# Hybrid decoder step on one core: two weight blocks kept for the late gates, and the first late gate moved ahead of two embeddings

## The reference, cut to what matters

```python
h = h + (p_l @ w_ple) * jax.nn.sigmoid(rmsnorm(h, g_ple) @ w_ple_gate)
...
y_prompt = rmsnorm(hp, g_final)
y_sample = rmsnorm(hs, g_final)
```

## Time and profile before

| what | value |
|---|---|
| runs | 2041.95, 2042.4, 2044.65 us; median 2042.4 us |
| profiled execution: its own time | 2045.19 us |
| its span (first to last instruction) | 2043.4 us |
| mean granted TensorE clock | 0.993 of full speed |
| TensorE matmul, busy share of the span | 98% |
| VectorE, ScalarE, GpSimd | 42%, 21%, 32% |
| gate pass with embeddings and output, from about | 1908 us to the end |

### The profile page before, as it was taken

The page is one execution under the profiler, slowest core; times in us unless marked ns, Lnnn a source line. Parts: engine busy times, 40 slices in busy tenths (PEclk is TensorE's granted clock), DMA queues, the critical chain, the costliest instruction groups (busy, mean ns, idle before and its releaser), DMA issues. The chain is left out here.

```text
span 2043.4 us, 34180 instructions
## 1 busy us (share of the span) xinstructions
PE 2005.5 (98%) x12890; PEld 1973.0 (97%) x12890; DVE 865.3 (42%) x1353; ACT 435.9 (21%) x842; POOL 663.4 (32%) x427
## 2 busy tenths in 40 slices
PE   7999999999999999999999999999999999999998
PEld 7999999989999999999999999999999999999998
DVE  4110434447256555644566543114212411344557
ACT  4111333321111222222232222002101200221312
POOL 5322232213322222224363232323232323232434
PEclk8999999999999999999999999999999999999999
DMA  7232122117444555577644111111111111111313
GB/s 199 75 92 52 37 63 63 57 44 206 114 139 133 152 163 166 176 131 220 196 133 161 44 42 52 41 52 41 52 41 51 41 51 41 51 42 51 104 50 128
DMA packets 251066, 191.43 MB, mean 94 GB/s; under 512 B 19116, under 2 KB 221976, under 8 KB 250594
## 3 DMA queue, kind: packets, MB, share of 16 engines
q1 hardware_dynamic: 241858, 172.27, 29.6%
q10 hardware_dynamic: 9120, 17.93, 2.8%
HBM read 157.10 MB, written 33.09 MB: 93 GB/s over the span
## 5 line engine op out<-in xcount | busy, mean ns | idle before, releaser
L142 PE MATMUL acc<-x_hi,w_hi 128*128 128x344 f32 x2496 | 809.0, 324 | 6.8 <-PEq L499 3.3
L142 PE MATMUL acc<-x_hi,w_lo 128*128 128x344 f32 x2496 | 799.2, 320 | 0.0
L142 PE MATMUL acc<-x_lo,w_hi 128*128 128x344 f32 x2496 | 798.9, 320 | 0.0
L112 POOL TENSOR_SCALAR w_hi<-w_raw 128x1024 fp32r<-128x1024 f32 (+1 forms) x176 | 182.6, 1037 | 1167.7 <-PE acc L142 995.3
L142 PEld LDWEIGHTS acc<-x_hi,w_hi 128*128 128x128 f32 x2496 | 471.1, 189 | 8.8 <-issue 7.7
L142 PEld LDWEIGHTS acc<-x_lo,w_hi 128*128 128x128 f32 x2496 | 470.9, 189 | 0.0
L142 PEld LDWEIGHTS acc<-x_hi,w_lo 128*128 128x128 f32 x2496 | 470.7, 189 | 0.0
L115 POOL TENSOR_TENSOR w_lo<-w_raw,w_hi 128x1024 fp32r<-128x1024 f32 (+1 forms) x176 | 411.6, 2338 | 14.7
L142 PE MATMUL acc<-z_hi,w_hi 128*128 128x344 f32 x768 | 245.9, 320 | 0.0
L142 PE MATMUL acc<-z_hi,w_lo 128*128 128x344 f32 x768 | 245.3, 319 | 0.0
L142 PE MATMUL acc<-z_lo,w_hi 128*128 128x344 f32 x768 | 245.1, 319 | 0.0
(11 more groups left out here) (297 smaller groups left out, 2060.2 us busy)
## 6 DMA issues: line engine op xcount, KB each, us to landing
w_raw<-in_w_in SPq DMA_DIRECT2D x64, 512.0 KB, 4.3
page<-in_cache_k SPq DMA_DIRECT2D x64, 256.0 KB, 3.0
page<-in_cache_v SPq DMA_DIRECT2D x64, 256.0 KB, 2.7
w_raw<-in_w_up SPq DMA_DIRECT2D x32, 512.0 KB, 4.0
w_raw<-in_w_down SPq DMA_DIRECT2D x32, 512.0 KB, 3.6
merge_gate<-merge_gates SPq DMA_DIRECT2D x22, 516.0 KB, 3.8
merge_gates<-gate_out ACTq DMA_DIRECT2D x18, 516.0 KB, 3.6
w_raw<-in_w_ple_gate SPq DMA_DIRECT2D x16, 512.0 KB, 3.6
```

The lines of the kernel that those rows point to most:

```text
L112: nc.gpsimd.tensor_scalar(k.w_hi[:, par, 0:kb, :], k.w_raw[:, par, 0:kb, :], 1.0, 1.0, ALU.mult, ALU.mult).then_inc(k.w_rounded, 1)
L142: mm = k.nc.tensor.matmul(k.acc[:, c, 0:CW], w[:, par, i, :], x[:, i, cols], start=(i == 0 and j == 0), stop=(i == kb - 1 and j == 2))
```

## The change

The early pass ends with blocks 6 and 7 in the two weight buffers. The late pass now takes the blocks in the order 6, 7, 0, 1, 2, 3, 4, 5, so that units 16 and 17 use what lies there, and blocks 0 to 5 are loaded again as j = 8 to 13. Two loads and two splits fall away. Block 8 is split behind gate 16, block 9 behind gate 17 (before: behind gates 13 and 15). Gate 16 is placed ahead of embeddings 14 and 15 on TensorE. VectorE's and ScalarE's lists stay as they are, but for the two conditions that ask whether a unit is the first of its columns, which now go by the unit's number. On SyncE's queue the loads of j = 10, 11 and 12 stand ahead of the first store, that of j = 13 between the first and the second. The last turning of tiles takes blocks 4, 6 and 7 first and block 5, the last one now, at the end.

```diff
-LATE = [(m, 2) for m in range(KD)]
+LATE_ORDER = [KD - 2, KD - 1] + list(range(KD - 2))
+LATE = [(m, 2) for m in LATE_ORDER]
...
             for m in range(KD):
-                if m + 2 < KD:
+                if m + 4 < KD:
                     gate_weights(KD + m + 2)
                 if m >= 2:
                     store(m - 2)
...
-            for j in range(2, 2 * KD):
-                pool.wait_ge(s["g_ready"], 2 * (j - 1) if j - 2 < KD else NE + j - 1 - KD)
+            for j in range(2, 2 * KD - 2):
+                pool.wait_ge(s["g_ready"], 2 * (j - 1) if j < KD else NE + j - KD + 1)
                 split_landed(k, pool, e0 + j, j % 2, (e0 + j) // 2)
...
-                j = m if u < NE else KD + m
+                j = m if u < NE + 2 else KD + m
...
+            gates(NE)
             embed(NE - 2)
             embed(NE - 1)
             for m in range(KD):
-                gates(NE + m)
+                if m:
+                    gates(NE + m)
...
+            LAST = LATE_ORDER[KD - 1:]
+            SECOND = [b for b in range(4, KD) if b not in LAST]
...
-            turn_half(pt[:, 0, :], a, range(4, KD - 1))
+            turn_half(pt[:, 0, :], a, SECOND)
...
-            turn_half(pt[:, 0, :], a, range(KD - 1, KD))
+            turn_half(pt[:, 0, :], a, LAST)
...
-                if m == 0:
+                if u < 2 or u == NE:
                     nc.vector.tensor_copy(sq3[:, cols], squares3[:, cols]).then_inc(s["sq_summed"], 1)
...
-                if m:
+                if u >= 2 and u != NE:
                     act.wait_ge(s["sq_summed"], same_columns_before(u) + 1)
```

More of the change, by code:

```diff
@@ L2089, in tensor @@
             pe.wait_ge(s["y_ready"], 2 * EARLY_TILES)
-            turn_half(pt[:, 0, :], a, range(4, KD - 1))
-            turn_half(pt[:, 1, :], b_, range(4, KD - 1))
+            turn_half(pt[:, 0, :], a, SECOND)
+            turn_half(pt[:, 1, :], b_, SECOND)
             pe.wait_ge(s["scaled"], NG)
-            turn_half(k.acc[:, 1, :], TB, range(4, KD - 1))
+            turn_half(k.acc[:, 1, :], TB, SECOND)
             pe.wait_ge(s["added"], NG)
-            turn_half(pt[:, 0, :], a, range(KD - 1, KD))
-            turn_half(pt[:, 1, :], b_, range(KD - 1, KD))
-            turn_half(k.acc[:, 1, :], TB, range(KD - 1, KD)).then_inc(s["half_turned"], 1)
+            turn_half(pt[:, 0, :], a, LAST)
+            turn_half(pt[:, 1, :], b_, LAST)
+            turn_half(k.acc[:, 1, :], TB, LAST).then_inc(s["half_turned"], 1)
             pe.wait_ge(s["sq_summed"], NG)
```

## The result

The changed kernel takes 2047.39 us (median of 20 runs) beside 2043.63 for the kernel before (20 runs); the ratio is 1.0018, with a 95% interval from 1.0012 to 1.0025. It is 2.5 to 5.1 us slower, where 0.9 slower was forecast. One of the changed kernel's 20 runs, 3302.13 us at a mean granted clock of 0.555, is left out of the ratio; without it the median is 2047.11.

A forecast was written before the change was run, and what follows sets the result against it. TensorE is busy nearly throughout; only two pauses, caused by a serial VectorE and ScalarE chain, can be won back. Chain +0.74, clock +0.7, late pass -0.5 gave +0.9: 2043.3 us for the median, range 2040.5 to 2045.8.

The forecast's parts named there:

- The steps of the chain: VectorE and ScalarE's serial work on units 12 to 15: 1.86 us won, 0.6 and 2.16 lost, token sums 0.74 later.
- Gate 16 without a wait: On TensorE, gate 16 follows embedding 13 at 1987.95 and runs until 1990.85, its weights and bank being ready.
- no pause before embedding 15: On TensorE, the 2.75 us wait for the product of unit 13 is gone.
- add 12 at 0.56: On VectorE, the add of unit 12 takes 0.56 in place of 2.42 without block 9's split: 1.86 us won.
- product 14 late: On VectorE, the product of unit 14 waits for its later embedding and starts at 1992.15 instead of 1991.56: 0.6 lost.
- add 14 held: On VectorE, block 8's w_lo half on GpSimd holds the add of unit 14 until 1995.46: 2.16 us lost.
- the token sums 0.71 later: On TensorE, the token sums start at 1998.86 where they started at 1998.12: 0.74 us later.
- a pause of 5.00: TensorE waits once before the token sums, from 1993.85 to 1998.86: 5.0 us instead of 2.75 and 1.28.
- The late pass: Fewer loads, in a new queue order, cut TensorE's 1.0 us wait for the y output: 0.5 won, ends 0 and 1.0.
- The clock's term: Low clock from 1998.0 costs the token sums 0.7 and gate 17 still 1.40: net +0.7, ends -1.4 and +2.9.
- rival 2: Slower: the 5.0 us pause keeps the clock low through token sums and all of gate 17: +3.6, 2046.0; chance 0.16.
- a cold gate 18: On TensorE, gate 18 also starts at the low clock: another 2.9, so 2048.9; thought unlikely.

The follow-up runs named there:

- e4: The changed kernel with block 8 split only behind the sum of unit 15; 2044.63 us, ratio 0.9998 to the kernel before.
- e1: The changed kernel's new block order, with gate 16 put back behind embedding 15; 2042.47 us, ratio 0.9991 to the kernel before.
- e2: The kernel before, in its old block order, with gate 16 moved ahead of embeddings 14 and 15; 2048.07 us, ratio 1.0019 to the kernel before.
- e5: The changed kernel with gate 17 moved ahead of the wait for the token sums; 2045.25 us, ratio 1.0011 to the kernel before.
- e11: The kernel before with gate 17 moved ahead of the wait for the token sums, nothing else; 2042.43 us, ratio 0.9996 to the kernel before.

## Why the prediction was wrong

- **The steps of the chain held.** Gate 16 without a wait, no pause before embedding 15, add 12 at 0.56, product 14 late (0.50 of waiting, 0.6 forecast), add 14 held (2.69 us from its start, 2.72 forecast), the token sums 0.71 later (0.74 forecast), a pause of 5.00 (5.0 forecast). e4 and e1 show the w_lo half as what holds add 14, by taking it away.
- **The late pass held.** TensorE's weight side waited 0.6 for the y output in place of 1.0, GpSimd waited for no load, and the part behind gate 17 took 0.65 less (0.5 forecast), of which those waits are 0.4; the rest isn't assigned.
- **The clock's term was mis-sized.** The prediction said "I take 0.7, the middle" for the token sums and kept "the 1.40 that the row shows" for gate 17, net +0.7. Measured: the token sums +1.22, close to the bound of 1.36, and gate 17 2.6 lost in place of 1.40, so +1.19; net +2.4. The error for the token sums was to take the middle of a bound where the text itself had the clock low before they began. The error for gate 17 was to carry over a loss that came from a low stretch of 3.4 us. After the change the stretch lasted 10.2 us, as it did in e2 and e5 (6.8 in e4 and e11), and it began 2.9 us behind the start of the pause, not 4.1. So the token sums took 2.72 us instead of 1.50, and gate 17 was cold to its end. This is rival 2, priced at +3.6 in the prediction and given 0.16; its price is inside the measured interval, and its further step, a cold gate 18, did not come.
- **The base.** The forecast stood on a median of 2042.4; over 20 runs it is 2043.63. Of the 1.6 us by which the range was missed, 1.2 are that.
- **What stays open.** The profiles differ by 2.47 us from the mark on, the medians by 3.8. The interval reaches down to 2.5, and e11 shows that the kernel before doesn't lose the same in each execution, but how the rest is divided was not measured.

The Trainium skill, TensorE: Matmul & The Clock Gate, section "HAM oscillation — how this bites in real kernels", was cited for cold work behind a wait. The runs agree: with the wait filled by useless matmuls the token sums went from 2.72 to 1.50 us. The prediction cited it and then priced the cold work at about half: 0.7 of at most 1.36 us, and 1.40 of at most 2.9.

## What to carry to other kernels

Work moved out from between two waits doesn't shorten the chain that both wait for; here it joined the two into one, and the clock then charged more than the wait. Before moving work into a gap, ask what covers the next gap, and price the work right behind a long pause as cold. In the profiles, one of each kernel, with 2.88 us or more of waiting just before the token sums (changed, e2, e4, e5) these took 2.72 us; with 1.28 or 1.30 (before, e1) they took 1.50 and only gate 17 was partly cold. A weight split on GpSimd belongs where no add with both inputs in SBUF, and no copy within it, is on the path: an order decided by 0.1 us was worth 2 us here.

## What the runs showed of the hardware

- Token sums of one column are nearly twice as long at 1.2 GHz (2.72 us for 1.50), though each matmul has one column.
- A copy with one SBUF input is held by GpSimd's w_lo half too, not only the adds with two: in e4 the copy of unit 16 took 1.88 us beside 0.30 in the changed kernel. The Trainium skill, SBUF — State Buffer, section "SBUF: two separate sides", names VectorE operations in a two-port performance mode, and a float32 copy within SBUF as one of them, among those that the lock on the pair of ports shared with GpSimd concerns; these rows agree.

```profile
1998.43 2.63 POOL L115 TENSOR_TENSOR w_lo<-w_raw,w_hi 128x1024 fp32r<-128x1024 f32 x1
```

```profile
1999.33 1.88 DVE L2192 COPY final_sums<-ple_prod 128x264 f32<-128x264 f32 x1 [0.49 <-ACT ple_prod L2295]
```

- A pause of about 2.75 us dropped the granted clock in one execution and not in another, with the same instructions ahead of it.
